# Moving the compressed branch to the score banks and starting the stick-breaking half's steps sooner

## The reference, cut to what matters

```python
s_c = einsum('bgrtd,bngd->bgrtn', q_t, k_cmp) * scale        # compressed: 32 keys
p_c = masked_softmax(s_c, mask_c)
o_cmp = einsum('bgrtn,bngd->bgrtd', p_c, v_cmp)
o = g[..., 0:1] * o_cmp + g[..., 1:2] * o_slc + g[..., 2:3] * o_win
```

```python
log_1m_beta = where(mask, log_sigmoid(-z), 0)
log_remain = cumsum(log_1m_beta, reverse=True) - log_1m_beta
att = where(mask, exp(log_beta + log_remain), 0)             # stick-breaking
x_r, x_k, x_v, x_w, x_a, x_g = split(u + (token_shift(u) - u) * mu)
decay = exp(-exp(log_w(w0 + tanh(x_w) @ w2)));  a = sigmoid(a0 + x_a @ a2)
kk = x_k * k_k / norm(...);  y = rwkv7_recurrence(r, decay, kf, v, -kk, kk * a)
```

## Time and profile before

| | |
|---|---|
| median of 3 runs | 1956.26 us (1955.57 to 1958.94) |
| the profiled execution | 1956.47 us, span 1954.7 us |
| granted TensorE clock, mean | 0.976 |
| TensorE busy | 1847.5 us, 95% |
| VectorE, ScalarE, GpSimd busy | 48%, 36%, 7% |

### The profile page before, as it was taken

The page is one execution under the profiler, slowest core; times in us unless marked ns, Lnnn a source line. Parts: engine busy times, 40 slices in busy tenths (PEclk is TensorE's granted clock), DMA queues, the critical chain, the costliest instruction groups (busy, mean ns, idle before and its releaser), DMA issues.

```text
span 1954.7 us, 27696 instructions
## 1 busy us (share of the span) xinstructions
PE 1847.5 (95%) x11652; PEld 1425.1 (73%) x11652; DVE 935.4 (48%) x1482; ACT 697.1 (36%) x1055; POOL 134.4 (7%) x109
## 2 busy tenths in 40 slices
PE   5999988979999999999999999899888999999999
PEld 3666655758888887688888877666788688888887
DVE  4367766364343343544244444545754644423442
ACT  3225546343223233433123334577311432312221
POOL 0023434200000002000000010000000010000000
PEclk8999989989999999899999999999999899999999
DMA  9772100113222222123222322111000222322231
GB/s 374 257 253 74 37 25 33 55 43 99 96 97 97 97 97 88 64 97 117 78 91 100 111 67 85 55 43 44 23 4 4 66 96 97 112 82 87 97 124 38
DMA packets 44475, 176.15 MB, mean 90 GB/s; under 512 B 5568, under 2 KB 5824, under 8 KB 41024
## 3 DMA queue, kind: packets, MB, share of 16 engines
q1 hardware_dynamic: 44352, 174.38, 25.8%
HBM read 168.33 MB, written 2.10 MB: 87 GB/s over the span
## 4 chain that ended last, share of the span: by engine, by line
PE 85%; DVE 6%; ACT 3%; DMA 3%; issue 2%; SPq 0%; POOL 0%; DVEq 0%; ACTq 0%
PE bank L363 24%; PE bank L365 23%; PE bank L364 23%; PE bank L523 1%; PE bank L539 1%; PE bank L507 1%; DMA arena<-ada_late 1%; PE bank L712 1%; DMA arena<-ada 1%; PE bank L853 1%; ACT arena L1195 1%; PE bank L870 1%; PE bank L861 1%; DMA ring<-m_w_v 1%; DVE arena L2046 1%
## 5 line engine op out<-in xcount | busy, mean ns | idle before, releaser
L1557 DVE TENSOR_TENSOR wsp<-ring,wsp 128x1024 fp32r<-128x1024 f32 (+2 forms) x244 | 312.3, 1282 | 448.5 <-ACT wsp L1084 448.4
L363 PE MATMUL bank<-hs,wsp 128*128 128x512 f32 x1160 | 473.3, 408 | 15.7 <-DVE hs L1823 5.3
L1084 ACT ACTIVATE wsp<-ring 128x1024 fp32r<-128x1024 f32 (+2 forms) x244 | 268.8, 1104 | 599.5 <-PE bank L365 593.3
L365 PE MATMUL bank<-hs,wsp 128*128 128x512 f32 x1160 | 455.8, 393 | 0.0
L364 PE MATMUL bank<-hs,wsp 128*128 128x512 f32 x1160 | 455.5, 393 | 0.0
L363 PEld LDWEIGHTS bank<-hs,wsp 128*128 128x128 f32 x1160 | 220.0, 190 | 87.5 <-issue 32.0
L364 PEld LDWEIGHTS bank<-hs,wsp 128*128 128x128 f32 x1160 | 220.2, 190 | 50.2 <-issue 6.0
L365 PEld LDWEIGHTS bank<-hs,wsp 128*128 128x128 f32 x1160 | 219.7, 189 | 47.4
L365 PE MATMUL bank<-hids,wsp 128*128 128x512 f32 x608 | 241.0, 396 | 0.0
L364 PE MATMUL bank<-hids,wsp 128*128 128x512 f32 x608 | 241.0, 396 | 0.0
L363 PE MATMUL bank<-hids,wsp 128*128 128x512 f32 x608 | 241.0, 396 | 0.0
(11 more groups left out here) (340 smaller groups left out, 2103.8 us busy)
## 6 DMA issues: line engine op xcount, KB each, us to landing
ring<-m_gate SPq DMA_DIRECT2D x44, 512.0 KB, 3.4
ring<-m_up SPq DMA_DIRECT2D x44, 512.0 KB, 3.4
ring<-m_down SPq DMA_DIRECT2D x32, 704.0 KB, 4.0
ring<-m_w_in SPq DMA_DIRECT2D x38, 512.0 KB, 3.4
arena<-ada_late SPq DMA_DIRECT2D x16, 1024.0 KB, 7.1
ring<-m_w_up SPq DMA_DIRECT2D x32, 512.0 KB, 3.4
ring<-m_w_down SPq DMA_DIRECT2D x32, 512.0 KB, 3.4
ring<-m_w_out SPq DMA_DIRECT2D x16, 512.0 KB, 3.6
```

Source lines behind the costliest of these rows:

```text
L363: pe.matmul(out, lhs[0], rhs[0], start=start, stop=False)
L365: return pe.matmul(out, lhs[1], rhs[0], start=False, stop=stop)
L1084: act.activation(wsp[:, s % SPLIT, 0, 0:size], ring[:, i % RING, 0:size], ACT.Copy)\
L1557: dve.tensor_tensor(wsp[:, s % SPLIT, 1, 0:size], ring[:, i % RING, 0:size], wsp[:, s % SPLIT, 0, 0:size].bitcast(F32), ALU.subtract).then ...
```

## The change

The compressed branch moves from banks 4 and 5 to the score bank that is free in that step and its neighbour, and its parts move to the end of the step. Three of its places and one output move by a step. In the late half `sb_step(0)` and `sb_step(1)` are called inside the value projection, all later steps five k earlier; Tanh, `rates`, `keys`, `decays` and `decayed` one round earlier and more; the four key norms, once in a row, are now one beside each `keys`; `first_products` go to rounds 10 to 13.

```diff
-        CMP_AT = [9, 12, 18, 26]
-        OUT_AT = [14, 19, 27, 35, 39, 43, 47, NP]
+        CMP_AT = [10, 13, 19, 26]
+        OUT_AT = [15, 19, 27, 35, 39, 43, 47, NP]
...
             def cmp_scores(i):
-                claim(4, "cmp_masked", i + 1)
-                claim(5, "cmp_masked", i + 1)
+                b = 1 + (2 * CMP_AT[i] + 2) % 3
+                claim(b, "cmp_masked", i + 1)
+                claim(b + 1, "cmp_masked", i + 1)
...
             def cmp_turn(i):
+                b = 1 + (2 * CMP_AT[i] + 6) % 3
                 pe.wait_ge(S("cmp_probs"), i + 1)
-                claim(4, "cmp_probT", i + 1)
+                claim(b, "cmp_probT", i + 1)
...
+                if p - 4 in CMP_AT:
+                    cmp_out(CMP_AT.index(p - 4))
+                if 2 <= p < NP + 2:
+                    turn_probs(p - 2)
+                if 3 <= p:
+                    pv(p - 3)
                 if p in CMP_AT:
...
                     cmp_scores(CMP_AT.index(p))
                 if p - 2 in CMP_AT:
                     cmp_turn(CMP_AT.index(p - 2))
-                if p - 4 in CMP_AT:
-                    cmp_out(CMP_AT.index(p - 4))
-                if 2 <= p < NP + 2:
-                    turn_probs(p - 2)
-                if 3 <= p:
-                    pv(p - 3)
```

TensorE's late half:

```diff
-            pe.wait_ge(S("qk2"), 8)
-            sb_step(0)
+            def beside_values(j):
+                if j == 0:
+                    head_norm(7)
+                if j == 1:
+                    pe.wait_ge(S("qk2"), 8)
+                    sb_step(0)
+                if j == 2:
+                    sb_step(1)
+
+            token_gemm("w_v2", 4, 2, T, "vtok2_full", "vtok2", VBANKS, beside_values)
...
-                    if (8 * n + k) % 5 == 4 and 8 * n + k < 5 * (PARTS + 1):
-                        sb_step((8 * n + k + 1) // 5)
-                    if (n, k) == (8, 2):
+                    if (8 * n + k) % 5 == 4 and 8 * n + k < 5 * PARTS:
+                        sb_step((8 * n + k + 1) // 5 + 1)
+                    if (n, k) == (7, 0):
                         rates(0)
                         rates(1)
-                    if (n, k) == (8, 4):
+                    if (n, k) == (7, 2):
+                        rates(2)
+                    if (n, k) == (7, 4):
+                        rates(3)
+                    if (n, k) == (7, 6):
                         osb_ms(3)
-                    if (n, k) == (8, 6):
-                        rates(2)
-                        rates(3)
...
-                if n >= 11:
-                    first_products(n - 11)
+                if n >= 10:
+                    first_products(n - 10)
```

```diff
+                if j == 2:
+                    act.wait_ge(S("qk2"), 8)
+                    sb_step(0)
+                if j == 3:
+                    sb_step(1)
+                    act.wait_ge(S("vtok2_full"), NT)
+                    values(0)
+                    values(1)
...
-                    if (n, k) == (8, 1):
+                    if (n, k) == (7, 0):
                         act.wait_ge(S("shifted"), 5)
                         act.activation(u[0:DH, UWA, :], u[0:DH, UWA, :], ACT.Tanh).then_inc(S("tanh"), 1)
-                    if (n, k) == (8, 2):
                         rates(0)
                         rates(1)
                         key_line(0)
-                        key_line(1)
-                    if (n, k) == (8, 6):
+                    if (n, k) == (7, 2):
                         rates(2)
+                    if (n, k) == (7, 4):
                         rates(3)
...
-                    if (n, k) == (9, 1):
                         decays(0)
+                        key_line(1)
+                    if (n, k) == (8, 0):
                         osb_root(3)
```

VectorE:

```diff
+                if k == 4:
+                    sb_mask(0)
+                if k == 5:
+                    softplus(0)
+                if k == 6:
+                    sb_step(1)
...
-                if n == 8:
+                if n == 7:
                     dve.wait_ge(S("sb_pv"), PARTS)
-                    for c in range(4):
-                        dve.wait_ge(S("kk_root"), c + 1)
...
                     scan(0)
+                    key_norm(0)
                     keys(0)
...
-                if 8 <= n < 12:
-                    decayed(n - 8)
+                if 7 <= n < 11:
+                    decayed(n - 7)
...
-                if 8 <= n < 11:
-                    scan(n - 7)
-                    keys(n - 7)
+                if 7 <= n < 10:
+                    scan(n - 6)
+                    key_norm(n - 6)
+                    keys(n - 6)
```

More of the change, by code:

```diff
@@ L385, in gemms, with token_gemm @@
                         sumsq(sums, k)
-            def token_gemm(name, tiles, kc, width, full, freed, at=(0, 1, 2, 3)):
+            def token_gemm(name, tiles, kc, width, full, freed, at=(0, 1, 2, 3), inside=None):
                 for t in range(NT):
@@ L406, in token_gemm @@
                         late_piece(j)
-                    if name == "w_v2" and j == 0:
-                        head_norm(7)
+                    if inside:
+                        inside(j)
             def sumsq(tag, k):
@@ L683, in _ @@
                     head_norm(n - 1)
-            token_gemm("w_v2", 4, 2, T, "vtok2_full", "vtok2", VBANKS)
             def set_of(p):
@@ L1314, in _ @@
                 own("qk_root")
-            def values(t):
-                act.activation(vtok2[:, t, :], bank[:, VBANKS[t], :], ACT.Identity, scale=rtok[:, t:t + 1]).then_inc(S("vtok2"), 1)
-                own("vtok2")
-            def values_read(j):
-                if j < 3:
-                    ahead("w_v2", j)
-                    act.wait_ge(S("w_v2_part"), j + 1)
-                else:
-                    act.wait_ge(S("vtok2_full"), NT)
-                    values(0)
-                    values(1)
-            norm_high("u")
-            values(2)
-            values(3)
-            ahead("w_v2", 3)
-            act.wait_ge(S("qk2"), 8)
             def sb_logs(p):
@@ L1409, in turned_values, with values, values_read @@
                                ACT.Copy).then_inc(S("vtk"), 1)
-            sb_step(0)
+            def values(t):
+                act.activation(vtok2[:, t, :], bank[:, VBANKS[t], :], ACT.Identity, scale=rtok[:, t:t + 1]).then_inc(S("vtok2"), 1)
+                own("vtok2")
+            def values_read(j):
+                if j < 3:
+                    ahead("w_v2", j)
+                    act.wait_ge(S("w_v2_part"), j + 1)
+                if j == 2:
[6 more added lines that the diff above has]
+                    values(1)
+            norm_high("u")
+            values(2)
+            values(3)
+            ahead("w_v2", 3)
             for n in range(14):
                 for k in range(KD):
-                    if (8 * n + k) % 5 == 4 and 8 * n + k < 5 * (PARTS + 1):
-                        sb_step((8 * n + k + 1) // 5)
-                    if (n, k) == (8, 1):
+                    if (8 * n + k) % 5 == 4 and 8 * n + k < 5 * PARTS:
+                        sb_step((8 * n + k + 1) // 5 + 1)
+                    if (n, k) == (7, 0):
                         act.wait_ge(S("shifted"), 5)
                         act.activation(u[0:DH, UWA, :], u[0:DH, UWA, :], ACT.Tanh).then_inc(S("tanh"), 1)
-                    if (n, k) == (8, 2):
                         rates(0)
@@ L1910, in _ @@
                 own("qk2")
-            def values_read(k):
-                if k in (0, 2, 4):
-                    ahead("w_v2", k // 2)
-            normalize("u", lambda k: vec("norm_mix_2", k), root=rmix, read=values_read)
-            ahead("w_v2", 3)
             def sb_mask(p):
@@ L1982, in scan, with key_norm @@
                 own("csum")
+            def key_norm(c):
+                dve.wait_ge(S("kk_root"), c + 1)
+                dve.scalar_tensor_tensor(out=knorm[:, c, :], in0=u[:, UK + c, :], scalar=vec("rw_k_k", c),
+                                         in1=u[:, UV + c, :], op0=ALU.mult, op1=ALU.mult).then_inc(S("knorm"), 1)
+                own("knorm")
             def keys(c):
@@ L2011, in bonus, with values_read @@
                 dve.tensor_tensor(u[:, UV + c, :], bank[:, 6 + c % 2, :], u[:, UV + c, :], ALU.mult).then_inc(S("bonus"), 1)
-            sb_step(0)
+            def values_read(k):
+                if k in (0, 2, 4):
+                    ahead("w_v2", k // 2)
+                if k == 4:
[4 more added lines that the diff above has]
+                    sb_step(1)
+            normalize("u", lambda k: vec("norm_mix_2", k), root=rmix, read=values_read)
+            ahead("w_v2", 3)
             for n in range(14):
                 for k in range(KD):
-                    if (8 * n + k) % 5 == 4 and 8 * n + k < 5 * (PARTS + 1):
-                        sb_step((8 * n + k + 1) // 5)
-                if n == 8:
+                    if (8 * n + k) % 5 == 4 and 8 * n + k < 5 * PARTS:
```

(8 more changed lines are left out.)

27 lines of the change are left out of this document (14 added, 13 removed).

## The result

The changed kernel takes 1964.7 us (median of 6 runs, 1962.45 to 1965.85). The kernel before, in the same measurement, took 1955.91 (median of 6, 1949.52 to 1958.94). The ratio is 1.0053, with a 95% interval of 1.0036 to 1.0069: slower by 7 to 13.5 us. Its profiled execution took 1965.85 us, with a span of 1964.1 us, 9.4 us over the span before.

The account below looks back on a forecast made before the run. TensorE was taken as the bound (85% of the chain), losing time to idle waits and low clock. Part one's -6.5 and part two's +13 gave +6.5 on 1956.47, so 1963 us, range 1950 to 1969.

Parts of the forecast that it names:

- Part two: Late half, with stick-breaking steps inside the values and Tanh, rates and rounds sooner: 13 us lost, bounds 4 and 19.
- Part one: Pair steps, with the compressed branch on new banks and places: 6.5 us won, bounds 1 and 23.
- the first two cases: First two places of the compressed branch: waits of 2.8 us against 4.0, no low clock, 2.5 us won together.
- the fourth case: Compressed branch from step 26: late scores and the copy leave 0 won, between 1 lost and 4 won.
- if no low clock follows, 3.3 more are won: Third case, steps 18 to 21: 3.3 us more without a low clock, some 1.8 with one; 4 us taken as won.
- The first softplus: First steps inside the values: wait of 8.0 us instead of 5.4, plus 0.75 for the read-out; 3.4 us lost.
- Tanh: Before `rates(0)`: TensorE waits 5.5 us instead of 1.7, 3.8 lost, plus a low clock of 1.7.
- The rounds: Heavy late rounds at VectorE's pace, a key norm in each: TensorE waits 9.8 us against 4.3, 5.5 lost.
- (1): Rival: part one wins its whole ceiling of 23 us, part two as forecast, 1946.5 us; 12%.
- (2): Rival: part two hardly loses, as the heavy rounds are hidden and the earlier start pays back, 1950 us; 12%.
- (3): Rival: both parts come out near nothing, the waits only change places, 1956.5 us; 14%.
- (4): Rival: the low clock stays through rounds 9 to 12, 1 us more in each and the last wholly slow, 1968; 8%.

Follow-up runs that it names:

- its repetition: The kernel before, run once more without any edit, for another trace: 1945.02 us in one run, pair steps 104.25 us.
- the chain ahead of the split: Changed kernel with the chain to the first softplus put before the weight split that waits for value tile 2: 1959.16 us, ratio 1.0033.
- one step moved so: Late half of before with only sb_step(0) inside the values, its chain ahead of the split, compressed parts at the step's start: 1942.48 us, ratio 0.9956.
- the compressed parts first: Kernel before with the compressed branch's new banks and steps, its scores, turn and output at the start of the step: 1950.19 us, ratio 0.9983.
- part one alone: Kernel before with only the compressed-branch edits in the pair steps, late half as before: 1953.05 us, ratio 0.9996.

## Why the prediction was right, and where it wasn't

**The sum.** 1963 was forecast and 1964.7 measured, slower, inside the range. Part two is right for the reason it gave: forecast at +13, it gave +12.9 alone. Part one is not: forecast at -6.5, it gave -0.8 (from 3.9 faster to 2.3 slower). By the parts alone the change would be 12.1 us slower where 6.5 was forecast; the two kernels side by side lie 8.8 us apart in their medians (7 to 13.5 by the ratio), and on a base 0.6 us under the one forecast from. So the right way and size of the change were reasoned out for part two, and that the number missed by only 1.7 us is in part luck.

**Part one.** Every wait came where it was put: 2.56 us for the scaling at step 21 (2.4 forecast), 3.50 at L507 for the copy at step 29 (3 to 4), 1.24, 0.75, 0.43 and 0.49 in the first two cases, 2.9 together (2.8 forecast). TensorE's idle time fell from 4.3 to 2.7 us in steps 18 to 21 (1.5 won by the forecast, 1.6 measured), from 4.04 to 3.25 in steps 9 to 17 (1.2 forecast, 0.8 measured), and not at all in the fourth case. The stretch of steps 18 to 21 took 21.97 us, over the 18 that would have spoken against part one; it had taken 23.32 in the trace before and 21.95 in its repetition, where 4 us were to be won. The step that failed is the price of the low clock, "if no low clock follows, 3.3 more are won" and the first two cases' "1.5 back": the 8.9 us of the earlier trace rows were taken as what the old waits cost, and they were what one execution paid. By the same working its repetition paid 0, 1.7 and 1.7, together 3.4 us (granted clock 1.00, 0.77 and 0.80). In other executions of the same instructions the pair steps are up to 4.9 us shorter. The profiled base, 109.17, was a long one. And at step 21 the low clock did follow the new wait, 0.50 over 3.0 us. The Trainium skill says in "TensorE: Matmul & The Clock Gate", section "HAM oscillation", that a long enough wait is paid with throttled time each time. Here the wait of 2.41 us was paid in one trace and not in another, and behind the one of 4.8 us the clock over the next 8.54 us was 0.52 in one and 0.80 in the other, so a fixed price per wait doesn't hold at these lengths, and the measurement decides. One reading of the rows is off as well: the compressed branch gives VectorE seven operations of 0.42 us per case, four and three, not six; the bursts of 1.8 us used in the sum are right.

**The first softplus.** The wait was to be 8.0 and was 7.84 (the terms listed for the chain add to 8.55, not 8.8, which would have made it 7.75); behind it 0.84 (0.75 forecast) for the read-out. The term was 3.4 and measured 4.6, because one wait was missing in it: 1.3 us of `kk_ms` for the root of an output norm, whose bank it shares and whose step had come closer.

**Tanh.** 4.96 against 5.5, 3.2 instead of 3.8 more than before. From the last exponential to the end of the load ScalarE took 1338.90 to 1345.32, 6.4 us where the terms summed to 6.7; the two table loads of 1.28 us, before Tanh and before the Sigmoids, stayed two. The low clock behind it came as forecast: the first four matmuls of the rates take 1.06 to 1.22 us against 0.59 to 0.69 before.

**The rounds.** Forecast were mixes at 16.2, 25.2, 35.0 and 44.0 us from the start of `rates(0)`. VectorE's timeline of the changed kernel has them at 17.6, 26.7, 36.6 and 45.7:

```profile
1363.65 0.74 DVE L1973 SCALAR_TENSOR_TENSOR arena<-bank,col,arena 128x511 f32<-128x511 f32 x1
...
1372.73 0.74 DVE L1973 SCALAR_TENSOR_TENSOR arena<-bank,col,arena 128x511 f32<-128x511 f32 x1
...
1382.60 0.74 DVE L1973 SCALAR_TENSOR_TENSOR arena<-bank,col,arena 128x511 f32<-128x511 f32 x1
...
1391.68 0.74 DVE L1973 SCALAR_TENSOR_TENSOR arena<-bank,col,arena 128x511 f32<-128x511 f32 x1
```

The paces, 9.1, 9.9 and 9.1 us, are those forecast; the start is 1.4 late. `scan(0)` is 1.9 late, at 8.5 instead of 6.6, but that costs nothing: VectorE then waits 3.74 us for ScalarE's split. ScalarE is late because it waits for the last output (0.59 us) and for `rates(3)` (0.74), which TensorE gives late, with a clock of 0.63 over the 5.4 us from 1346.01. The three waits add to 6.4 us, not 9.4, and the 0.4 at `rates(2)` didn't come. This is the mis-sized term, and it moved no time: VectorE sets the pace, and TensorE, at 0.50 from 1374.70 to 1377.30 and from 1384.25 to 1387.20, was busy for longer instead. Tanh, rates and rounds together were 9.6 in the forecast (3.8 + 1.7 + 5.5 - 0.6 - 0.8) and measured 9.0.

**The rivals.** (1), the ceiling of 23 us, never came near. (2) fails at part two's 12.9. (3), places changed for nothing, comes near what part one alone does, but not part two. (4), the low clock through all rounds, did not happen: the stretch from 1348.3 to 1393.4 has 0.91, lower than the 0.96 of the earlier trace rows, but not low throughout.

## What to carry to other kernels

A step moved ahead is only worth what its longest chain lets it: count from the instruction that starts the chain, on each engine behind what else it has queued there, to the one that needs its end. Here one tile of other work between was 3.3 us too little even with the chain ahead of the split, and two tiles and five k left 6.6 us to spare; one step moved so won 6.3 us of the late stretch, where the whole group moved lost 13.6. When one engine sets the pace of a group of rounds, sum that engine's work to cost the rounds: the forecast from VectorE's work was right to 0.6 us, while TensorE's waits were 3 us less than forecast. And before a saving is read off one trace, find out with a second trace of the same program whether the stretch repeats, and read idle time apart from busy time: here the idle time repeated to 0.05 us where the length differed by 4.9.

## What the runs showed of the hardware

The same wait of 2.41 us, at the same instruction with the same work before it, was followed by a granted clock of 0.50 over 2.95 us in one execution and 1.00 in another. Four executions of the same pair steps took 104.25 to 109.17 us, with TensorE idle for 14.05 to 14.09 of them, while the new pair steps took 105.29 to 105.76 in six traces, and the late stretch 180.84 to 181.03 in four traces of its old form though it has waits of 5.4 and 3.4 us. A low clock needs no wait of 2 us before it: with the compressed parts first it was 0.50 over 3.0 us (214.50 to 217.50) where the last waits were 0.78 and 0.57 us. In the late rounds waits of 3.08 and 2.03 us were followed by a low clock and one of 1.24 was not. Within one kernel the runs spread over some 15 us (1945.17 to 1960.04 for part one alone).
